# Attention with shared keys: two rounds of scores behind every second query tile, the softmax, transposes and values one step later

## The reference, cut to what matters

```
# dilated_attention
q = (x @ w_q).reshape(bsz, s, N_GROUPS, N_HEADS, HEAD_DIM).astype(jnp.float32)
for g, (window, dilation) in enumerate(DILATION_PAIRS):
    o, l = dilated_group(q[:, :, g], k, v, slopes, window, dilation)
    ...
wts = jax.nn.softmax(jnp.stack(lses, axis=0), axis=0)
out = jnp.sum(wts[..., None] * jnp.stack(outs, axis=0), axis=0)
return out.reshape(bsz, s, N_HEADS * HEAD_DIM).astype(x.dtype) @ w_o

# dilated_group: causal, query t attends keys t, t-d, ..., t-window
scores = jnp.where(valid[:, None], scores + bias, NEG_INF)
m = jnp.max(scores, axis=-1, keepdims=True)
p = jnp.exp(scores - m)
denom = jnp.sum(p, axis=-1, keepdims=True)
lse = (m + jnp.log(denom))[..., 0]
out = jnp.einsum("bpnhqk,bpnkhd->bpnqhd", p / denom, vw)
```

## Time and profile before

| | |
|---|---|
| Median of 3 runs | 1741.24 us (1741.16 to 1741.4) |
| The profiled execution, its own time | 1741.44 us |
| Its span in the profile | 1739.3 us |
| Busy: TensorE / VectorE / ScalarE | 98% / 71% / 56% of the span |
| DMA | mean 166 GB/s, 50% of the 16 engines' time on the hardware queue |
| Granted TensorE clock, mean | 0.997 |

### The profile page before, as it was taken

One profiled execution on the slowest core, in us unless ns is written; L12 is line 12 of the kernel. 1 busy time (PEld: TensorE's weight loads), 2 busy tenths in 40 slices (PEclk: granted clock), 3 DMA queues, 4 the chain that ended last, 5 costly groups with the idle time before them and its releaser, 6 DMA issues.

```text
span 1739.3 us, 33419 instructions
## 1 busy us (share of the span) xinstructions
PE 1712.3 (98%) x11808; PEld 1559.0 (90%) x11808; DVE 1234.7 (71%) x2175; ACT 975.8 (56%) x1710; POOL 30.0 (2%) x24
## 2 busy tenths in 40 slices
PE   9999998999999999999899999999999999999998
PEld 7888998888899888888788888989999999898887
DVE  6777789777664776677687766868655567787765
ACT  6564596655454655466566544565533356666543
POOL 0000000000000000000000000000000000000000
PEclk9999999999999999999999999999999999999999
DMA  7566455456544656433355564234455543345562
GB/s 229 191 200 197 136 182 180 148 183 202 191 150 159 196 191 221 154 122 122 98 214 192 192 202 150 98 121 135 148 177 189 182 125 135 112 149 190 192 202 89
DMA packets 76350, 288.82 MB, mean 166 GB/s; under 512 B 9312, under 2 KB 11616, under 8 KB 76256
## 3 DMA queue, kind: packets, MB, share of 16 engines
q1 hardware_dynamic: 76256, 287.53, 50.0%
HBM read 286.45 MB, written 1.05 MB: 165 GB/s over the span
## 4 chain that ended last, share of the span: by engine, by line
PE 91%; DVE 4%; ACT 2%; issue 1%; DMA 0%; SPq 0%; ACTq 0%; DVEq 0%
PE psum L534 33%; PE psum L535 17%; PE psum L526 11%; PE psum L528 10%; PE psum L527 10%; PE psum L572 1%; PE psum L784 1%; PE psum L622 1%; PE psum L567 1%; PE psum L568 1%; DVE wlo L1586 1%; PE psum L669 1%; ACT whi L1111 1%; PE psum L886 0%; DVE r_sq L1754 0%
## 5 line engine op out<-in xcount | busy, mean ns | idle before, releaser
L1586 DVE TENSOR_TENSOR wlo<-raw,whi 128x1024 fp32r<-128x1024 f32 (+2 forms) x490 | 636.6, 1306 | 286.1 <-ACT whi L1111 285.1
L534 PE MATMUL psum<-x_split,whi 128*128 128x512 f32 x1696 | 592.9, 393 | 2.4 <-DVE x_split L1621 2.4
L1111 ACT ACTIVATE whi<-raw 128x1024 fp32r<-128x1024 f32 (+2 forms) x494 | 545.5, 1116 | 37.8 <-PE psum L528 13.9
L535 PE MATMUL psum<-x_split,wlo 128*128 128x256 f32 x1696 | 475.6, 280 | 0.0
L534 PEld LDWEIGHTS psum<-x_split,whi 128*128 128x128 f32 x1696 | 318.3, 188 | 75.7 <-DVE x_split L1621 2.5
L535 PEld LDWEIGHTS psum<-x_split,wlo 128*128 128x128 f32 x1696 | 318.7, 188 | 0.0
L526 PE MATMUL psum<-x_split,whi 128*128 128x272 f32 (+1 forms) x1072 | 311.8, 291 | 0.0
L528 PE MATMUL psum<-x_split,wlo 128*128 128x272 f32 (+1 forms) x1072 | 306.4, 286 | 0.0
L527 PE MATMUL psum<-x_split,whi 128*128 128x272 f32 (+1 forms) x1072 | 305.5, 285 | 0.0
L534 PE MATMUL psum<-h_split,whi 128*128 128x512 f32 x770 | 272.1, 397 | 0.0
L535 PE MATMUL psum<-h_split,wlo 128*128 128x256 f32 x770 | 216.1, 281 | 0.0
(11 more groups left out here) (237 smaller groups left out, 1869.1 us busy)
## 6 DMA issues: line engine op xcount, KB each, us to landing
raw<-w_in SPq DMA_DIRECT2D x264, 512.0 KB, 3.3
raw<-w_out SPq DMA_DIRECT2D x96, 704.0 KB, 4.2
raw<-w_mix SPq DMA_DIRECT2D x42, 512.0 KB, 3.3
raw<-w_rg SPq DMA_DIRECT2D x25, 512.0 KB, 3.5
raw<-w_q SPq DMA_DIRECT2D x24, 512.0 KB, 3.3
raw<-w_kv SPq DMA_DIRECT2D x16, 512.0 KB, 3.3
raw<-w_mixo SPq DMA_DIRECT2D x16, 512.0 KB, 3.3
raw<-w_rg_out SPq DMA_DIRECT2D x8, 640.0 KB, 4.0
```

Source lines behind the costliest of these rows:

```text
L534: nc.tensor.matmul(ps[:, bank, :], whi[slot][:, w], split, start=start, stop=False)
L535: return nc.tensor.matmul(part(bank, 0), wlo[slot][:, w], split[:, 0], start=False, stop=stop)
L1111: nc.scalar.activation(whi[slot][:, 0:cols], raw[slot][:, 0:cols], ACT.Copy).then_inc(w_hi_done, count)
L1586: V.tensor_tensor(wlo[slot][:, 0:cols], raw[slot][:, 0:cols], f(whi[slot][:, 0:cols]), ALU.subtract).then_inc(w_lo_done, 1)
```

## The change

TensorE no longer makes one round after each query tile: at every even step from 2 to 24 it makes two, S(s-2) and S(s-1), in all four score banks. VectorE takes two biases at every odd step. Everything behind (exps, sums, transposes, copies, values, output) comes one step later in each engine's program. The steps at which `begin_output` stands are not moved, nor is the loading of weights.

```diff
@@ TensorE
-            for s in range(Q_TILES + 6):
+            for s in range(Q_TILES + 7):
...
-                if 1 <= s <= Q_TILES:
+                if 2 <= s <= Q_TILES and s % 2 == 0:
+                    scores(s - 2)
                     scores(s - 1)
-                if s >= 6 and s % 3 == 0:
-                    transposed(2 * (s // 3 - 2))
-                if s >= 6 and s % 3 == 1:
-                    transposed(2 * (s // 3 - 2) + 1)
-                if s >= 6 and s % 3 == 2:
-                    values(s // 3 - 2)
+                if s >= 7 and s % 3 == 1:
+                    transposed(2 * ((s - 7) // 3))
+                if s >= 8 and s % 3 == 2:
+                    transposed(2 * ((s - 8) // 3) + 1)
+                if s >= 9 and s % 3 == 0:
+                    values((s - 9) // 3)
@@ ScalarE
-            for s in range(Q_TILES + 7):
+            for s in range(Q_TILES + 8):
                 if s < Q_TILES:
                     round_ahead(st, s // SLOTS, s % SLOTS)
+                if s >= 9 and s % 3 == 0:
+                    copy_transposed(2 * ((s - 9) // 3) + 1)
+                if s >= 10 and s % 3 == 1:
+                    round_output((s - 10) // 3)
                 if s >= 8 and s % 3 == 2:
-                    copy_transposed(2 * ((s - 8) // 3) + 1)
-                if s >= 9 and s % 3 == 0:
-                    round_output((s - 9) // 3)
-                if s >= 7 and s % 3 == 1:
-                    copy_transposed(2 * ((s - 7) // 3))
-                if 5 <= s < Q_TILES + 4 and s % 3 == 2:
-                    exps(2 * ((s - 5) // 3))
-                if 6 <= s < Q_TILES + 4 and s % 3 == 0:
-                    exps(2 * ((s - 6) // 3) + 1)
+                    copy_transposed(2 * ((s - 8) // 3))
+                if 6 <= s < Q_TILES + 5 and s % 3 == 0:
+                    exps(2 * ((s - 6) // 3))
+                if 7 <= s < Q_TILES + 5 and s % 3 == 1:
+                    exps(2 * ((s - 7) // 3) + 1)
@@ VectorE
-            for s in range(Q_TILES + 7):
+            for s in range(Q_TILES + 8):
                 if s < Q_TILES:
                     rest(s)
-                if 2 <= s < Q_TILES + 2:
+                if 3 <= s < Q_TILES + 2 and s % 2:
+                    bias_max(s - 3)
                     bias_max(s - 2)
-                if 5 <= s < Q_TILES + 4 and s % 3 == 2:
-                    sum_groups(2 * ((s - 5) // 3))
-                if 6 <= s < Q_TILES + 4 and s % 3 == 0:
-                    sum_groups(2 * ((s - 6) // 3) + 1)
-                if s >= 9 and s % 3 == 0:
-                    rest_of_output((s - 9) // 3)
+                if 6 <= s < Q_TILES + 5 and s % 3 == 0:
+                    sum_groups(2 * ((s - 6) // 3))
+                if 7 <= s < Q_TILES + 5 and s % 3 == 1:
+                    sum_groups(2 * ((s - 7) // 3) + 1)
+                if s >= 10 and s % 3 == 1:
+                    rest_of_output((s - 10) // 3)
```

## The result

The changed kernel takes 1746.95 us (median of 10 runs, 1745.02 to 1749.14). Runs of the kernel before beside it gave 1741.83 (10 runs). The ratio is 1.0024, with a 95% interval of 1.0016 to 1.0032: slower, by 5.1 us in the medians (the interval is 2.8 to 5.6 us). 1746.1 was forecast.

What follows compares the result with a forecast made beforehand. TensorE was taken to bound the query steps, and the softmax chain the drain. From 1741.44 us, 2.15 net for the drain's waits after the pairs' saving and 2.5 for the clock gave 1746.1 us, range 1744.8 to 1747.5.

Steps and rivals of the forecast that it cites:

- The pairs' saving: Query steps on TensorE: a second round adds 0.66 us, each pair saves about 0.31, eleven pairs before step 24 save 3.4.
- The rival that a second round costs 0.86: Query steps: the second round starts over, each of 12 pairs saves 0.20 us less, total 1748.5 us; chance 0.12.
- No new stop in the query steps: Query steps: VectorE's paired biases stay covered by other TensorE work, closest call about 1 us to spare; priced at nothing.
- Step 24: Start of the drain on TensorE: expected at 844.6 us, against 849.74 before.
- the first idle: Drain, TensorE idle after V(5) until rest(5) is done: expected 4.3 us, ending at 852.6.
- The waits of the drain: TensorE idles 4.3 and 4.8 us at steps 25 and 28; the drain takes back the saving plus 2.15 us.
- The rival that the delay is hidden: Drain: the extra step costs nothing and the pairs' saving stays, total 1737.7 us, faster; chance 0.08.
- The clock: Drain: the granted clock falls to half behind each of two new idles, 1.25 us each, 2.5 us together.
- the prediction's steps: The drain's numbered timeline of engine work from step 24, ending with the last O at 868.1 us, at full clock.
- The rival of a clock that costs nothing: Drain: the clock holds, or falls while nothing runs, total 1743.6 us; chance 0.22.
- the fall in the earlier trace: Recurrent block before the change: half clock from 277.0 to 280.3 us after a 2.06 us idle, taken to cost 1.5.
- The sum: Whole kernel: profiled 1741.44 us plus 2.15 for the drain and 2.5 for the clock, 1746.1 us.

Runs made afterwards that it cites:

- shift_only: The changed kernel with one round and one bias at each step again, so the step of delay without the pairs: 1751.08 us, ratio 1.0049.
- warm: The changed kernel with 29 and 34 dummy matmuls into free banks in TensorE's two drain idles: 1744.01 us, ratio 1.0010.
- hybrid: The kernel before with rounds 0 to 19 in pairs and head pairs 0 to 4 one step later, the rest at old steps: 1739.70 us, ratio 0.9984.
- before_order: The kernel before with O(1, 0 to 2) ahead of O(0, 3 to 5), and later output products behind T(15) and V(7): 1740.57 us, ratio 0.9991.
- pairs_best: The kernel before with paired rounds, no delay, later output products, and nine dummy matmuls ahead of transposes 14 and of 15: 1737.29 us, ratio 0.9969.
- after_order: The changed kernel with its output products moved to where their inputs are ready, no output wait ahead of transposes 12 and 13: 1741.04 us, ratio 0.9994.
- pairs_only: The kernel before with rounds and biases in pairs, everything else at its old step, without the delay: 1740.18 us, ratio 0.9987.
- pairs_order: The kernel before with paired rounds and biases, no delay, and output products moved later: 1738.66 us, ratio 0.9977; run again, 1738.08 us, 0.9975.

## Why the prediction was right

**The pairs' saving: right.** A pair takes 808.89 - 807.38 = 1.51 us to the next work, where 0.86 + 0.66 = 1.52 was the sum. So what a change of form costs is paid once for both rounds, and by experiment (shift_only to changed) a pair is worth 0.30 us. Six steps take 807.38 - 782.31 = 25.07 us, so three take 12.54 (12.55 forecast). The rival that a second round costs 0.86 is refuted.

**No new stop in the query steps: right.** TensorE waits for nothing from the first wait to the last query tile.

**Step 24: 0.5 us off.** It starts at 846.52, which is 845.13 with the start of the attention set to 755.42, and 844.6 was forecast. I missed a wait. O(0, 0 to 2) may not start before the last query tile is copied, and T(11) alone (845.75) covers less of that copy than a round and a values did. The missed half microsecond then vanished in the idle behind V(5), because the chain through VectorE didn't pass through it: rest(5) came at 853.47 - 1.39 = 852.08, forecast 852.1. For the same reason the first idle was 3.81 and not 4.3.

**The waits of the drain: right.** They sit where they were put, at steps 25 and 28, ended by `h_split`, at 3.81 and 4.76 us (4.3 and 4.8 forecast), and cost 2.12 us net of the pairs (2.15 forecast; warm). The rival that the delay is hidden is refuted by shift_only.

**The clock: right in kind, its size too low.** The term was 2.5 us, with 1.5 for each idle as its upper bound. It measured 2.9 in the medians and 4.2 in the profiled execution. The first low stretch cost 1.5: from the restart to T(13) 858.06 - 853.95 = 4.11 instead of the 2.6 of the prediction's steps. The second lasted for 6.8 us, twice the one in the earlier trace rows, and cost 2.7: to T(15) 870.45 - 865.16 = 5.29 instead of 2.9, and 1.42 from there to V(7) instead of 1.1. I had priced only one length, and the second is outside my bound. That the median lies in the range owes something to luck: with 4.2 the sum would be 1747.8, above my 1747.5. The rival of a clock that costs nothing is refuted by warm.

The price itself was read from a place that doesn't show it. I wrote that the fall in the earlier trace rows cost 1.5 us. TensorE's products did run 1.5 us longer there, but the next wait took that up. The changed kernel has the same idle in the same unchanged block, with the clock at full behind it. The first line is of before, the others of the changed kernel (timeline, and the stretch as in the earlier trace rows):

```profile
283.00 0.38 PE L526 MATMUL psum<-h_split,whi 128*128 128x256 f32 x1 [0.71 <-DVE h_split L1856]
```
```profile
278.40 0.35 PE L526 MATMUL psum<-h_split,whi 128*128 128x256 f32 x1 [2.06 <-DVE h_split L1857]
...
284.35 0.58 PE L526 MATMUL psum<-h_split,whi 128*128 128x256 f32 x1 [2.17 <-DVE h_split L1857]
```
```profile
278.40:281.80 3.40, 3.40 (x29) 3.40 (x30) 3.37 (x5) 0.56 (x1) 0.00 (x0) 1.00 0.47 124
```

From one wait to the next it is 5.95 us in both (277.05 to 283.00, 278.40 to 284.35), and only the idle at the end differs, 0.71 against 2.17. So a low stretch costs time only where TensorE's work is on the chain. In the drain it is, and there 1.5 for a stretch of this length was right.

**The sum.** 1746.1 against 1746.95. Of the difference 0.4 is the clock (2.9 for 2.5) and as much the level of the runs of before beside it (1741.83, where the sum began at 1741.44). This split is no finer than the half microsecond or so by which the clock's cost in the medians is uncertain.

## What to carry to other kernels

An instruction that waits blocks everything behind it on its engine, so when a chain is moved one step later, ask for each consumer left at its old step what now stands behind its wait. Here the loss came from output products ahead of the transposes that the longest chain needed. A step of delay cost nothing here while other work covered it, and in waits 2.12 + 3.62 = 5.7 us at the end, so a saving per step has to be weighed against that drain, or the last iterations keep the old schedule. And try each half of a change alone: the pairing didn't need the delay.

## What was not expected of the hardware

The same idles left the clock at full in one execution and lowered it in another. In its drain the kernel before idles 1.23 us and 0.97 us, and between them, which the prediction left out, 1.59:

```profile
860.95 0.38 PE L526 MATMUL psum<-h_split,whi 128*128 128x256 f32 x1 [1.59 <-DVE h_split L1938]
```

Its clock stays at 1.00. The hybrid idles 1.23 and 1.58 us at the same places, and the clock stands at 0.50 for the 3.4 us behind the second. In the drain such a stretch cost 1.3 to 1.5 us. The recurrent block is the same in all kernels, and shows it without any change of program. Behind the same idle, of 2.00 to 2.06 us, the clock fell in the profiled executions of before, hybrid, before_order and pairs_best, and stayed at full in the other seven.

The table has this in it. The profiled executions of shift_only, the changed kernel and after_order hold low stretches in the drain that bring the clock to 0.83 over 849 to 880, hybrid, pairs_only, before_order and both of pairs_order one (0.94), and before, warm and pairs_best none. So the attention's length should be compared only between executions with the same number of them, or with their cost taken off. What decides whether an idle of this size lowers the clock these runs don't show.
